# One core of a two-block transformer: attended values from loaded value columns, modulation shared with TensorE, other places for the projection's operands

## The reference

```python
c_act = silu(c)
for i in range(2):                              # first block
    mod = c_act @ ada_w[i] + ada_b[i]           # 1024 x 6144: six rows of 1024
    sh1, sc1, g1, sh2, sc2, g2 = split(mod, 6)
    h = rmsnorm(x, norm_mix_g[i]) * (1 + sc1) + sh1
    y = pool_mixer(h) if i == 0 else sgu_mixer(h)
    x = x + g1 * y
    h = rmsnorm(x, norm_mlp_g[i]) * (1 + sc2) + sh2
    x = x + g2 * (square(relu(h @ w1[i])) @ w2[i])      # 1024 -> 4096 -> 1024
x = rmsnorm(x, final_g)

h = rms_norm(x, norm_mix_pre)                   # second block
q, k, v, p = split(h @ w_in, (512, 640, 768))
attn = sliding_window_sink_attention(q, k, v)   # 8 query heads, 2 key heads of 64, window 128
rw = rwkv7_time_mix(shifted p)                  # 8 heads of 64, a recurrence over the tokens
x = x + rms_norm(concat(attn, rw) @ w_out, norm_mix_post)
x = x + rms_norm(conv_gated_ffn(rms_norm(x, norm_ffn_pre)), norm_ffn_post)

# attention, of each block of 128 tokens with the 128 keys before it and its own
m = maximum(scores.max(-1), sink)
p = exp(scores - m)
out = (p / (p.sum(-1) + exp(sink - m))) @ v
```

## Time and profile before

| | |
|---|---|
| median of 3 runs | 1869.09 us |
| the profiled execution | 1869.46 us, of it the span 1868.1 us |
| PE busy | 1788.6 us (96%) |
| DVE busy | 1029.7 us (55%) |
| ACT busy | 644.3 us (34%) |
| POOL busy | 68.0 us (4%) |
| mean granted clock of PE | 0.974 |

### The profile page before, as it was taken

How to read it: one execution, slowest core, us unless ns; L and a number is a source line. 1 busy time by engine, 2 the same in 40 slices (tenths; PEclk the granted TensorE clock), 3 DMA queues, 4 the chain that set the end, 5 groups by cost and what they waited for, 6 DMA issues and landing times. The chain is left out here.

```text
span 1868.1 us, 21661 instructions
## 1 busy us (share of the span) xinstructions
PE 1788.6 (96%) x8926; PEld 1471.7 (79%) x8926; DVE 1029.7 (55%) x1343; ACT 644.3 (34%) x819; POOL 68.0 (4%) x87
## 2 busy tenths in 40 slices
PE   6679999999999899999999989999899999999998
PEld 4468888888788688888887877887788888888887
DVE  6975774477455543234347575565556642465533
ACT  4233213421333442133245423444444431344422
POOL 0100010010000000000000010110000000000000
PEclk9789999999899899999999998999999999999999
DMA  9842663266222223322332250002232233223221
GB/s 374 315 154 72 217 231 115 91 225 214 80 90 91 68 91 93 110 91 91 106 97 79 68 113 21 4 2 91 81 111 91 90 96 108 90 91 111 92 91 68
DMA packets 124146, 210.70 MB, mean 113 GB/s; under 512 B 14109, under 2 KB 48565, under 8 KB 124048
## 3 DMA queue, kind: packets, MB, share of 16 engines
q1 hardware_dynamic: 115520, 177.03, 29.0%
q0 software_dynamic: 8384, 31.70, 4.8%
q10 hardware_dynamic: 144, 0.59, 0.1%
HBM read 206.14 MB, written 4.73 MB: 113 GB/s over the span
## 5 line engine op out<-in xcount | busy, mean ns | idle before, releaser
L1750 DVE TENSOR_TENSOR w_lo<-raw,w_hi 128x2048 fp32r<-128x2048 f32 x138 | 316.3, 2292 | 468.8 <-ACT w_hi L1268 468.7
L1268 ACT ACTIVATE w_hi<-raw 128x2048 fp32r<-128x2048 f32 x138 | 263.9, 1912 | 574.0 <-PE bank L559 567.3
L559 PE MATMUL bank<-h_hi,w_hi 128*128 128x512 f32 x736 | 294.4, 400 | 14.2 <-DVE h_lo L1797 9.3
L559 PE MATMUL bank<-h_lo,w_hi 128*128 128x512 f32 x736 | 290.4, 395 | 0.0
L559 PE MATMUL bank<-h_hi,w_lo 128*128 128x512 f32 x736 | 290.1, 394 | 0.0
L559 PE MATMUL bank<-u_hi,w_hi 128*128 128x512 f32 x512 | 200.7, 392 | 0.0
L559 PE MATMUL bank<-u_hi,w_lo 128*128 128x512 f32 x512 | 199.4, 389 | 0.0
L559 PE MATMUL bank<-u_lo,w_hi 128*128 128x512 f32 x512 | 199.2, 389 | 0.0
L559 PE MATMUL bank<-f_hi,w_hi 128*128 128x512 f32 x496 | 193.0, 389 | 0.0
L559 PE MATMUL bank<-f_lo,w_hi 128*128 128x512 f32 x496 | 193.0, 389 | 0.0
L559 PE MATMUL bank<-f_hi,w_lo 128*128 128x512 f32 x496 | 192.9, 389 | 0.0
(11 more groups left out here) (385 smaller groups left out, 2394.3 us busy)
## 6 DMA issues: line engine op xcount, KB each, us to landing
raw<-in_mlp_w SPq DMA_DIRECT2D x128, 512.0 KB, 4.6
raw<-in_w_ffn_up SPq DMA_DIRECT2D x64, 512.0 KB, 4.6
ada_ring<-in_ada_w SPq DMA_DIRECT2D x12, 2048.0 KB, 17.7
ada_ring<-in_ada_w POOLq DMA_DIRECT2D x24, 1024.0 KB, 5.5
raw<-in_w_ffn_down SPq DMA_DIRECT2D x32, 512.0 KB, 4.5
raw<-in_w_in SPq DMA_DIRECT2D x20, 512.0 KB, 4.3
raw<-in_sgu_w_in SPq DMA_DIRECT2D x16, 512.0 KB, 4.9
raw<-in_sgu_w_out SPq DMA_DIRECT2D x8, 512.0 KB, 4.7
```

Of the source, the lines that this page charges most:

```text
L559: mm = te.matmul(bank[:, n], a, b, start=first and k == 0 and j == 0, stop=last and k == 3 and j == 2, skip_group_check=s == SLABS["ffn"] + 1)
L1268: se.activation(m.ring(s)[0], m.raw[:, slot], ACT.Copy).then_inc(sem("hi_made"), 1)
L1750: ve.tensor_tensor(lo, m.raw[:, slot], hi.bitcast(F32), ALU.subtract).then_inc(sem("lo_made"), 1)
```

## The change

**Modulation.** Of the eight row blocks of a group DVE adds six; the last two are added by PE in the same PSUM columns (`ada_rows`, eight matmuls with one moving column, c[k]). This holds for groups 0 to 9. Groups 10 and 11 stay on DVE, in other places, with `w_lo` of the next slab ahead of group 11.

**The mixer.** A unit of attention takes two heads of each key head instead of four of one; its scores alternate between the two halves of the array's rows. The probabilities are divided by DVE before they are turned (`scaled`), one unit ahead. `values` keeps 64 columns of v stationary and moves 256 columns of probabilities, so that the result comes out transposed and `attn_back` and `a_rows` go. The scores have two buffers. `probs` stands behind `inverse_t`, `values` behind `inverse_end`.

**Places.** The projection's operands have places of their own (`am_hi`, `am_lo` for attention, `om_hi`, `om_lo` for RWKV), and `w_lo` of its first slab has one that is free earlier.

```diff
@@ -150,6 +150,8 @@
 ADA_ORDER = (2, 0, 3, 1, 4, 5, 6, 8, 7, 9, 10, 11)
 ADA_SLOT = (0, 1, 2, 3, 0, 1, 2, 3, 0, 2, 1, 3)
...
+
+ADA_SUMMED = (6,) * 10 + (8,) * 2
...
+    def ada_rows(i):
+
+        g, slot = ADA_ORDER[i], ADA_SLOT[i]
+        if i == 0:
+            te.wait_ge(sem("silu_made"), MILESTONE["silu_made"])
+        if i >= 2:
+            te.wait_ge(sem("mod_made"), i - 1)
+        te.wait_ge(sem(f"ada_in{slot}"), 16 * ADA_SLOT[:i + 1].count(slot))
+        for k in range(ADA_SUMMED[i], 8):
+            for c in range(4):
+                te.matmul(bank[:, 6 + i % 2, 4 * g + c:4 * g + c + 1], m.ada_ring[:, slot, k, P * c:P * c + P], m.c_act[:, k:k + 1],
+                          start=k == ADA_SUMMED[i] and c == 0, stop=False, skip_group_check=True)
+
     def ada_sums(i):
 
         g, slot = ADA_ORDER[i], ADA_SLOT[i]
-        te.wait_ge(sem("ada_step"), 8 * i + 8)
-        if i >= 2:
+        te.wait_ge(sem("ada_step"), sum(ADA_SUMMED[:i + 1]))
+        if i >= 10:
             te.wait_ge(sem("mod_made"), i - 1)
         for c in range(4):
             a = m.ada_ring[:, slot, 0, P * c:P * c + P] if i < 10 else m.ada1_acc[:, 2 * (i % 2) + c // 2, P * (c % 2):P * (c % 2) + P]
-            mm = te.matmul(bank[:, 6 + i % 2, 4 * g + c:4 * g + c + 1], a, ones[:, 0:1], start=True, stop=True)
+            mm = te.matmul(bank[:, 6 + i % 2, 4 * g + c:4 * g + c + 1], a, ones[:, 0:1], start=i >= 10 and c == 0, stop=True,
+                           skip_group_check=True)
         mm.then_inc(sem("ada_columns"), 1)
...
-    mix_pool(6)
     mix_pool(7)
+    ada_rows(6)
...
-                            ada_sums(8)
+                        if k == 0 and kk:
+                            ada_rows(7 + kk)
                     starting = layer == 0 and half == 0 and g == 0
                     slab(s + k, group, m.h_hi[:, 4 * k:4 * k + 4], m.h_lo[:, 4 * k:4 * k + 4], k == 0, k == 1,
                          before_k if half == 0 and g == 0 else None, before_n, k_outer=starting,
                          after_k=after_k if starting else None)
                     if starting and k == 0:
+                        ada_sums(8)
                         ada_sums(9)
                 if layer == 0 and half == 0 and g == 2:
...
 
     def scores(it):
-        n, half = divmod(it, 2)
+        n, i0 = it // 2, 2 * (it % 2)
         j0 = 128 if n == 0 else 0
-        r0 = 64 * half
         b = wide("scores", it)
-        for i in range(4):
-            mm = te.matmul(bank[:, b + i // 2, 256 * (i % 2) + j0:256 * (i % 2) + 256],
-                           m.qT[r0:r0 + 64, i, P * n:P * n + P], m.kT[r0:r0 + 64, P * n - P + j0:P * n + P],
-                           start=True, stop=True)
+        for ii in range(2):
+            for half in range(2):
+                rr = halves[half]
+                mm = te.matmul(bank[:, b + half, 256 * ii + j0:256 * ii + 256],
+                               m.qT[rr, i0 + ii, P * n:P * n + P], m.kT[rr, P * n - P + j0:P * n + P],
+                               start=True, stop=True)
         mm.then_inc(sem("wide_full"), 1)
 
     def probs(it):
...
+                mm = te.transpose(bank[:, b + q, P * i:P * i + P], m.scores[:, it % 2, i, P * q:P * q + P], ident)
         mm.then_inc(sem("wide_full"), 1)
 
     def values(it):
-        n, half = divmod(it, 2)
+        n = it // 2
         te.wait_ge(sem("wide_emptied_act"), WIDE_EMPTIED[WIDE_AT["probs", it]][1])
         if it:
             te.wait_ge(sem("attn_taken"), it)
-        for i in range(4):
-            for q in range(n == 0, 2):
-                mm = te.matmul(bank[:, 7, 64 * i:64 * i + 64], m.p_t[:, q, i], m.v_rows[:, n - 1 + q, 64 * half:64 * half + 64],
+        for q in range(n == 0, 2):
+            for half, rr in enumerate(halves):
+                mm = te.matmul(bank[rr, 7, 0:256], m.v_rows[:, n - 1 + q, rr], m.p_t[:, q, 2 * half:2 * half + 2].rearrange("p i t -> p (i t)"),
                                start=q == (n == 0), stop=q == 1)
         mm.then_inc(sem("attn_summed"), 1)
-
...
-        inverse_copies(u)
+        inverse_copy(u)
+        probs(u)
+        end_copy(u)
         if not last:
             rows(u + 1)
-            exps(u + 1, (0, 1))
+            exps(u + 1, range(4))
+            if u == UNITS - 2:
+                for n in range(3):
+                    attn_hi(n)
             key_values(u + 1)
...
             gates()
-        if last:
-            for j in range(4):
-                x_rowed(j)
-            se.wait_ge(sem("attn_summed"), UNITS)
-            split_to(SLABS["w_out"])
-            se.wait_ge(sem("unit_used"), UNITS)
-            for n in range(3):
-                attn_hi(n)
-        if u % 2:
-            n = u // 2
-            b = wide_full("attn", n)
-            se.activation(m.attnT[:, :, P * n:P * n + P], bank[:, b].rearrange("p (i t) -> p i t", i=4), ACT.Copy).then_inc(sem("wide_emptied_act"), 1)
...
@@ -1944,7 +1961,12 @@
         for half in range(2):
             for g in range(4):
                 s = s0 + 16 * half + 2 * g
+                early = layer == 0 and half == 0
+                if early and g == 2:
+                    ada(11)
                 split_to(s + 2)
+                if early and g == 0:
+                    ada(10)
                 for n in range(4):
                     tile = 32 * layer + 16 * half + 4 * g + n
                     ve.wait_ge(sem("act_emptied"), EMPTIED[g0 + 6 * half + g][n][1])
@@ -1952,8 +1974,11 @@
                     ve.wait_ge(sem("relu_squared"), tile + 1)
                     ve.wait_ge(sem("u_hi_made"), tile + 1)
                     ve.tensor_tensor(u_lo[:, 4 * g + n], sq[:, n], u_hi[:, 4 * g + n].bitcast(F32), ALU.subtract).then_inc(sem("u_lo_made"), 1)
-                if layer == 0 and half == 0:
-                    late(g)
+                if early and g < 2:
+                    split_to(s + 3)
+                elif early and g == 3:
+                    mod(10)
+                    mod(11)
             for g in range(2):
                 s, group = s0 + 16 * half + 8 + 4 * g, g0 + 6 * half + 4 + g
                 for k in range(4):
...
+    def scaled(it):
+
+        j0 = 128 if it < 2 else 0
+        s, sm = m.scores[:, it % 2, :, j0:], m.small[:, it % 2]
+        ve.wait_ge(sem("scores_exped"), it + 1)
+        n = own.on(ve.tensor_tensor(sm[:, 3], sm[:, 3], sm[:, 4], ALU.add))
+        ve.wait_ge(own.sem, n)
+        n = own.on(ve.reciprocal(sm[:, 3], sm[:, 3]))
+        ve.wait_ge(own.sem, n)
+        ve.tensor_tensor(s, s, sm[:, 3].unsqueeze(2).broadcast_to([P, 4, 256 - j0]), ALU.mult).then_inc(sem("probs_scaled"), 1)
+
     def take(it):
 
-        n, half = divmod(it, 2)
-        sm = m.small[:, half]
-        ve.wait_ge(sem("scores_exped"), it + 1)
-        n1 = own.on(ve.tensor_tensor(sm[:, 3], sm[:, 3], sm[:, 4], ALU.add))
-        ve.wait_ge(own.sem, n1)
-        n1 = own.on(ve.reciprocal(sm[:, 3], sm[:, 3]))
-        ve.wait_ge(own.sem, n1)
+        n, i0 = it // 2, 2 * (it % 2)
         ve.wait_ge(sem("attn_summed"), it + 1)
-        if n and half == 0:
-            ve.wait_ge(sem("wide_full"), WIDE_AT["attn", n - 1] + 1)
-        ve.tensor_tensor(m.a_rows[:, :, half], bank[:, 7, 0:256].rearrange("p (i d) -> p i d", i=4),
-                         sm[:, 3].unsqueeze(2).broadcast_to([P, 4, 64]), ALU.mult).then_inc(sem("attn_taken"), 1)
+        ve.tensor_copy(m.attnT[:, i0:i0 + 2, P * n:P * n + P], bank[:, 7, 0:256].rearrange("p (i t) -> p i t", i=2)).then_inc(sem("attn_taken"), 1)
 
     def masked(name, u, to, mask):
         slot = m.block(u)[2]
...
@@ -2441,26 +2486,23 @@
         if u in O_STATS:
             o_stats(O_STATS.index(u))
         unit_ends(u)
+        if last:
+            split_to(SLABS["w_out"])
         state(u, 0)
+        if last:
+            attn_lo(3)
+        else:
+            scaled(u + 1)
         if u in O_BACK:
             o_gated(O_BACK.index(u))
```

More of the change, by code:

```diff
@@ L235, in rings @@
             stack, place = stage(self)
-            self.rings.append((place(f"w_hi{n}", [P, 2, 4, 512], FR), place(f"w_lo{n}", [P, 2, 4, 512], FR)))
+            hi, lo = place(f"w_hi{n}", [P, 2, 4, 512], FR), place(f"w_lo{n}", [P, 2, 4, 512], FR)
+            self.rings.append(((hi[:, 0], hi[:, 1]), (lo[:, 0], lo[:, 1])))
             return stack
@@ L653, in mix_pool @@
         mm.then_inc(sem("pool_full"), 1)
+    ada_rows(0)
+    for k in range(DT):
+        if k >= 4:
+            te.wait_ge(sem("x_copied"), k - 3)
+        for j in range(4):
+            if k == 0:
+                te.wait_ge(sem(f"x_in{j}"), 16)
+            mm = te.transpose(bank[:, k % 4, P * j:P * j + P], m.x_rows[:, j, P * k:P * k + P], ident)
+        mm.then_inc(sem("x_turned"), 1)
     ada_sums(0)
@@ L657, in tensor_program @@
         windows(k)
+        if k == 3:
+            ada_rows(1)
         if k == 5:
@@ L2286, in wide_full, with by_key_head @@
         return 2 * (x % 2)
+    def by_key_head(a):
```

(24 more changed lines are left out.)

164 lines of the change are left out of this document (78 added, 86 removed).

## The result

| | before | changed |
|---|---|---|
| median, us | 1869.01 (4 runs, 1866.58 to 1870.45) | 1845.78 (4 runs, 1842.74 to 1846.31) |
| profiled execution, us | 1869.46, span 1868.1 | 1842.74, span 1841.4 |
| PE busy | 1788.6 | 1787.7 |
| mean granted clock | 0.974 | 0.979 |

The ratio is 0.9874, with an interval of 0.9859 to 0.9890: 23.2 us faster.

A forecast was written before the change was run, and what follows sets the result against it. PE was taken as the bound, busy 96% of the span: waits decide in the start, PE's work in the mixer. Start -7.3, mixer -11.2 and its end -0.6 sum to -19.1: 1850.0 us, range 1842 to 1862.

The forecast's parts named there:

- First norm: Start: first norm row about 4.0 us earlier, 9.2 gained on DVE less 5.1 lost to half clock.
- bill: Start: PE's work from 33.35 to the first norm row, 36.5 us, leaving PE no slack.
- three such stretches: Start, up to the first norm: three half-clock stretches of some 3.4 us, each costing 1.7, together 5.1 us.
- the prediction's own sign: Start: the prediction is wrong if the first norm comes after 81.5.
- Second norm: Start, groups 8 and 9: PE is last instead of DVE; costs 1.4 us, taken as 2 for the clock.
- First tiles: Start: the fourth slab's w_lo comes sooner; 3.5 us of wait and a 1.7 half-clock stretch go, -5.3 with rounding.
- Scores and values: Mixer, PE: scores at a pair's 1.07 and values at 1.05 us; each saves about 4.7 us in all.
- The end of the mixer: Before the projection: a 3.75 us wait goes, against a 2.5 stall and a 1.7 half-clock stretch; net -0.6.
- Full clock throughout: Rival, chance 0.13: PE's denser queue stays at full clock, the start gives -13.1, total 1844 us.
- Halves that don't overlap: Rival, chance 0.12: scores stay at 1.71, values cost 1.7; 8.6 of the mixer's 11.2 us are lost: 1859.
- Loads: Rival, chance 0.08: groups 4 to 7 in the start wait for their loads, the norm's gain goes: 1855 us.
- Slower: Rival, chance 0.05: one-column matmuls hold PE at 1.2 GHz through the whole start: 1880 us.

The follow-up runs named there:

- all steps on DVE: Changed kernel with all eight steps of every group on DVE: 1848.10 us; the same with unit 6's gate behind the second state copy: 1843.25 us.
- one half: Changed kernel with the scores' four matmuls in one half of the array's rows and, from unit 2, the values' on one half of the output's partitions: 1856.18 us.
- four row blocks: Changed kernel with four of eight row blocks on PE instead of two, for groups 0 to 9: 1885.89 us, ratio 1.0082.
- `w_lo` late: Changed kernel with w_lo of the projection's first slab made after the last unit's states, as before the change: 1852.02 us.
- extra pass: Changed kernel with one more DVE pass over the 1024 columns behind each division of the probabilities: 1853.98 us.

## Why the prediction was right, point by point

**The total.** Forecast 1850.0 with 1842 to 1862; measured 1845.78. The sum was -19.1; the median moved by 23.2, the profiled run by 26.7: -7.7 in the start (forecast -7.3), -2.3 in the untouched middle (none), -16.7 in mixer and projection (-11.8). The middle's 2.3 and 2.5 of the mixer's (below) are where the clock happened to fall.

**First norm: the bill right, the clock's term mis-sized.** PE has no slack left, as the bill said. The prediction's own bill, 36.5 us of PE work behind 33.35, ends at 69.85 at the full clock. The changed kernel had a mean granted clock of 0.80 from there to its first norm row, which is 9.2 us lost in 45.95: 79.0 by the bill, 79.30 measured. The step that was off is "I take three such stretches ... 5.1": 9.2 and not 5.1 were lost. It was also taken from the 9.2 that DVE alone could gain, where the bill let PE gain 11.7. The two errors partly cancel: forecast 4.0, measured 2.2.

One number also stood for a distribution. Seven profiled executions have the same list up to the norm. Their first norm rows come at 77.38, 77.57, 79.30, 79.41, 82.76, 85.96 and 86.02, and their 8th slabs from 161.1 to 170.1, with granted clocks of 0.88 down to 0.77 between 24 and 77. The bill with each one's clock up to its norm row (6.6 to 16.9 us lost) meets all seven within 1.2 us, so the clock is what tells them apart. Three of the seven are later than 81.5, which by the prediction's own sign would have made it wrong; that the changed kernel's profile was not one of them is luck. Its other three runs are within 3.6 us of the profiled one, so by their totals they weren't either, but that is inferred.

With all steps on DVE the norm row came at 80.67 and 81.42. The shared steps thus buy nothing that these runs can show; that the groups' 9.2 us at the full clock are there is shown by no run. Whether they also add the spread is not shown by two profiles of the other kind.

**Second norm.** Forecast +2, measured +0.2 (100.36 less 79.30 against 102.39 less 81.53). The first two terms together were forecast at -2.0 and came out at -2.0, by luck.

**First tiles.** Forecast -5.3, measured -5.7 (from the second norm to the 8th slab). The wait of 4.4 went altogether.

**Scores and values: right.** 0.97 and 1.02 where 1.07 and 1.05 were taken, and it is the two halves at work together that do it (one half: 1.72 and 1.9). The rule on drains at a change of mode (the Trainium skill, "TensorEngine Tiling (Array Packing)", "Key Properties") costs no more than is inside these numbers.

**The units and the lead-in: the work right, the clock a draw.** They gave 14.1 where 11.2 was forecast. In the execution with before's clock pattern in the lead-in and unit 0 (four row blocks) they gave 11.6, near the forecast. The other 2.5 are half-clock work that the changed kernel's profile did not have there: 3.9 us of it instead of 10.5. Eight of the twelve profiles with the new mixer are like it and four are not; both profiles with the old mixer have the long pattern. The prediction had no term for it, and what decides it stays open.

**The end of the mixer.** At the projection the forecast counted one stretch more (+1.7). There was one less behind `m_lo`'s wait and one more behind the stall of 2.04, so it was nothing: -2.6 measured, -0.6 forecast. The run with `w_lo` late brings the wait back at that very place, and half-clock work behind it. The stretch behind the stall is less sure: it followed in six of the seven profiles with a stall of 2.04 or 2.05, not in the seventh, and not behind the 3.42 of the extra pass.

**The stalls of DVE's division: right.** 2.04 in the last unit (forecast 2.5), 0.29 in unit 5 (0.6), none elsewhere.

**The rivals.** Full clock throughout: by no run; the best had 0.88. By the Trainium skill's rule ("TensorE: Matmul & The Clock Gate", "What's actually happening") activity releases the clock; here 15.15 busy us of 16 stood at 0.52, so that in this stretch a stream of mostly one-column matmuls, busy as the profile counts it, did not release it. Halves that don't overlap: excluded. Loads: L640 waits for one only ahead of x. Slower: it needed more one-column work, and four row blocks bring it. (That rival's sum starts at 34.4 where the bill starts at 33.35; it would be 1879 by the bill.)

What stays open: what decides, from run to run of one list, where the clock falls, in the start, in the middle and ahead of unit 0.

## What to carry to other kernels

Moving work from a waiting engine's supplier onto the engine itself turns its waits into work, and then its clock sets the time beside its instruction count; compare several executions before one such stage is priced. A wait removed on TensorE can be worth more than its length where a stretch at half the clock stood behind it. Count that half as a chance, not as a certainty, and look at other executions of the same instructions before a half-clock stretch that has gone is booked as the change's gain. Where a stationary or an output is only 64 wide, spread the matmuls over both halves of the array; their order within a group of four made no difference here.

## What the runs showed of the hardware

- Four fp32 matmuls of 256 columns take 0.96 to 1.03 us in two halves of the array and 1.72 (scores) to 1.9 (values) in one, and it made no difference whether the halves took turns or came two and two. It fits an engine that starts on the other half while a matmul of the first is not done; the runs don't show how far ahead.
- One-column matmuls: eight cost 1.7 at the full clock and 3.4 at half; they keep PE busy in the profile (53.00 of 53.00 us) while the granted clock goes down.
- One list of instructions, seven executions: a stage of about 80 us differs by 8.6 us, and the granted clock accounts for it to 1.2 us. With the extra pass the whole kernel's runs fall in two groups 9 us apart (1848.7 and 1849.4, 1858.5 and 1858.6); with `w_lo` late they spread over 12 us.
- Ahead of the mixer's unit 1, the same instructions (slightly others in one) ran at the lower level for 3.7 to 4.2 us of PE's busy time in eight executions and for 9 to 14 in four; between two of them it made 2.5 us. Behind a wait of 2.04 or 2.05 in the last unit a half-clock stretch followed in six of seven executions, behind one of 3.42 in none of one, behind one of 1.01 in none of four.
